# Hybrid attention and delta-rule block: one block transpose read straight from PSUM, and four steps of the per-pair chain moved to later quarters

## The reference

```python
proj = h @ w_in + b_in                      # 2048 x 14880
aq, ak, av, dq, dk_, dv_, dz, db, da, ga, gb = split_cols(proj, IN_SPLITS)
o_att = sliding_window_sink_attention(rope(aq), rope(ak), av, att_sinks)
q, k, v = causal_depthwise_conv(dq|dk_|dv_) -> silu; q, k L2-normalised per head
# gated delta rule, chunked: a = (k_beta k^T) * decay * strict, solve (I + a) sol = rhs
qk = einsum(q, k) * decay;  k_dec = k * exp(gcum[-1] - gcum)
o_dn = gated_rms_norm(o_dn, dz, dn_norm_g)
merged = sigmoid(ga) * (o_att @ w_br_att) + sigmoid(gb) * (o_dn @ w_br_dn)
h = layer_norm(ALPHA * h + merged @ w_out)
h = layer_norm(ALPHA * h + swiglu(h) + sigmoid(h @ w_ple_gate + b) * (p @ w_ple_proj))
```

## Time and profile before

| | us |
|---|---|
| median of 3 runs | 1945.42 |
| lowest, highest | 1945.41, 1946.96 |
| the profiled execution, own time | 1945.95 |
| its span in the trace | 1944.0 |
| PE busy in it | 1912.1 (98%) |
| DVE busy | 1272.8 (65%) |
| ACT busy | 1026.6 (53%) |
| turns 1 to 7 of `mixer_turn` | period 66.1 each |

### The profile page before, as it was taken

One profiled execution on the slowest core, in us unless ns is written; L12 is line 12 of the kernel. 1 busy time (PEld: TensorE's weight loads), 2 busy tenths in 40 slices (PEclk: granted clock), 3 DMA queues, 4 the chain that ended last, 5 costly groups with the idle time before them and its releaser, 6 DMA issues.

```text
span 1944.0 us, 29842 instructions
## 1 busy us (share of the span) xinstructions
PE 1912.1 (98%) x10549; PEld 1662.1 (86%) x10549; DVE 1272.8 (65%) x2348; ACT 1026.6 (53%) x2068; POOL 37.5 (2%) x79
## 2 busy tenths in 40 slices
PE   8999999999999999999999999999999999999997
PEld 7889999999999888888888788888888888888886
DVE  6657888888888756565666697555555555555555
ACT  4446666666656545455444564545444444444442
POOL 1000000000000000000000000000000000000000
PEclk9999999999999999999999999999999999999999
DMA  8665555455445557566566455655555565655552
GB/s 312 194 161 195 116 144 118 136 135 135 112 144 122 183 163 248 195 200 200 191 213 224 153 195 196 200 187 194 193 183 186 193 194 177 230 197 195 195 195 87
DMA packets 203604, 349.65 MB, mean 180 GB/s; under 512 B 6704, under 2 KB 72448, under 8 KB 202512
## 3 DMA queue, kind: packets, MB, share of 16 engines
q1 hardware_dynamic: 200272, 334.26, 52.2%
q0 software_dynamic: 3264, 14.47, 5.2%
HBM read 344.32 MB, written 2.10 MB: 178 GB/s over the span
## 4 chain that ended last, share of the span: by engine, by line
PE 89%; DVE 5%; ACT 3%; issue 3%; DMA 0%; DVEq 0%; ACTq 0%; SPq 0%
PE dense L573 23%; PE dense L574 23%; PE dense L575 23%; PE dense L561 4%; PE dense L562 4%; PE dense L563 4%; PE chain L717 1%; DVE lo L1374 1%; ACT hi L1029 1%; PE chain L799 1%; ACT sE L1207 1%; PE chain L984 0%; PE chain L726 0%; DMA raw<-in_w_in_dram 0%; PE chain L817 0%
## 5 line engine op out<-in xcount | busy, mean ns | idle before, releaser
L1374 DVE TENSOR_TENSOR lo<-raw,hi 128x512 fp32r<-128x512 f32 x1256 | 852.8, 691 | 519.8 <-ACT hi L1029 517.3
L1029 ACT ACTIVATE hi<-raw 128x512 fp32r<-128x512 f32 x1256 | 777.4, 630 | 634.6 <-PE dense L575 604.9
L573 PE MATMUL dense<-hi,xh 128*128 128x512 f32 x1376 | 539.8, 392 | 1.5 <-DVE xl L1918 1.1
L575 PE MATMUL dense<-lo,xh 128*128 128x512 f32 x1376 | 536.0, 390 | 0.0
L574 PE MATMUL dense<-hi,xl 128*128 128x512 f32 x1376 | 535.7, 389 | 0.0
L573 PEld LDWEIGHTS dense<-hi,xh 128*128 128x128 f32 x1376 | 258.7, 188 | 55.2 <-DVE xl L1918 2.0
L575 PEld LDWEIGHTS dense<-lo,xh 128*128 128x128 f32 x1376 | 258.4, 188 | 54.4
L574 PEld LDWEIGHTS dense<-hi,xl 128*128 128x128 f32 x1376 | 258.6, 188 | 52.2
L561 PE MATMUL dense<-xh,hi 128*128 128x256 f32 x1024 | 303.2, 296 | 0.0
L563 PE MATMUL dense<-xh,lo 128*128 128x256 f32 x1024 | 289.4, 283 | 0.0
L562 PE MATMUL dense<-xl,hi 128*128 128x256 f32 x1024 | 289.2, 282 | 0.0
(11 more groups left out here) (309 smaller groups left out, 1516.4 us busy)
## 6 DMA issues: line engine op xcount, KB each, us to landing
raw<-in_w_in_dram SPq DMA_DIRECT2D x116, 1024.0 KB, 5.1
raw<-in_w_ffn_gate_dram SPq DMA_DIRECT2D x44, 1024.0 KB, 5.0
raw<-in_w_ffn_up_dram SPq DMA_DIRECT2D x44, 1024.0 KB, 5.1
raw<-in_w_ffn_down_dram SPq DMA_DIRECT2D x44, 1024.0 KB, 5.0
raw<-in_w_br_att_dram SPq DMA_DIRECT2D x16, 1024.0 KB, 5.0
raw<-in_w_br_dn_dram SPq DMA_DIRECT2D x16, 1024.0 KB, 5.0
raw<-in_w_out_dram SPq DMA_DIRECT2D x16, 1024.0 KB, 4.9
raw<-in_w_ple_gate_dram SPq DMA_DIRECT2D x16, 1024.0 KB, 5.0
```

What stands on the lines that cost most here:

```text
L573: pe.matmul(o, ah, hi[:, s, :], start=(k == 0), stop=False)
L575: mm = pe.matmul(o, ah, lo[:, s, :], start=False, stop=(k == nk - 1))
L1029: act.activation(hi[:, pos.slot(n), :], raw[:, slot, off:off + 512], ACT.Copy).then_inc(sem("hi_ready"), 1)
L1374: dve.tensor_tensor(lo[:, pos.slot(n), :], raw[:, slot, off:off + 512], hi[:, pos.slot(n), :].bitcast(F32), ALU.subtract).then_inc(sem("lo ...
```

## The change

In PE's stream the turning of q goes from stage 4 to stage 6 (quarter 6 to 8). On ACT the squares of q go from stage 5 to stage 7 (quarter 7 to 9), and the copies into `Um` at stage 15 wait for `t_rows` in place of `x_prod`. On DVE the mask of q k^T goes from stage 1 to stage 4 (quarter 1 to 6), the decayed keys from stage 2 to stage 8 (quarter 2 to 10), the four transposes of neighbour blocks from stage 13 to stage 14 (quarter 15 to 16), and the transpose at stage 15 waits for `x_prod` itself and reads PSUM where it read `Um`. No instruction is added or taken away, but for waits.

```diff
--- before.py
+++ after.py
@@ chain_stage, PE
-                elif k == 4:
+                elif k == 6:
                     q_to_rows(p)
@@ chain_k, ACT
-                elif k == 5:
+                elif k == 7:
                     act.wait_ge(sem("q_rows"), p + 1)
                     act.wait_ge(sem("k_sum"), p + 1)
@@ inverse_k, ACT
                 elif k == 15:
-                    act.wait_ge(sem("x_prod"), nth("x_prod", 5, p))
+                    act.wait_ge(sem("t_rows"), p + 1)
                     for q in range(0, 4, 2):
                         r = act.activation(Um[quadrant(q), :, quadrant(q + 1)],
                                            C[quadrant(q), 0, 0:P].rearrange("p (x c) -> p x c", x=4), ACT.Copy)
@@ inverse_k, DVE
-                elif k == 13:
+                elif k == 14:
                     dve.wait_ge(sem("vu_out"), nth("vu_out", 4, p))
                     for q in range(0, 4, 2):
                         a = dve.transpose(Yz[quadrant(q + 1), 0, :, quadrant(q)], flat(VU[quadrant(q), 1]))
@@
                 elif k == 15:
-                    dve.wait_ge(sem("u_other"), p + 1)
-                    dve.transpose(Tm[quadrant(1), :, quadrant(0)],
-                                  Um[quadrant(0), :, quadrant(1)]).then_inc(sem("t_rows"), 1)
+                    dve.wait_ge(sem("x_prod"), nth("x_prod", 5, p))
+                    dve.transpose(Tm[quadrant(1), :, quadrant(0)], C[quadrant(0), 0, 0:P]).then_inc(sem("t_rows"), 1)
@@ chain_k, DVE
                 elif k == 1:
-                    dve.wait_ge(sem("E"), p + 1)
-                    dve.wait_ge(sem("QKp"), p + 1)
-                    dve.wait_ge(sem("silv"), p + 1)
-                    dve.tensor_tensor(flat(QKT[:]), C[:, 1, :], flat(Em[:]), ALU.mult).then_inc(sem("QKm"), 1)
                     dve.wait_ge(sem("k_sum"), p + 1)
@@
                 elif k == 2:
                     dve.wait_ge(sem("KK"), p + 1)
+                    dve.wait_ge(sem("E"), p + 1)
                     dve.wait_ge(sem("b_scale"), p + 1)
@@
                     a.then_inc(sem("ATc"), 1)
-                    dve.wait_ge(sem("k_sum"), p + 1)
+                elif k == 8:
                     dve.tensor_tensor(kd[:], C[:, 2, :].rearrange("p (h t c) -> p h t c", h=2, t=TT)[:, :, 0, :],
                                       each(kdecs[:, 0, ds(2 * p, 2)], 2), ALU.mult).then_inc(sem("kdec"), 1)
                 elif k == 4:
+                    dve.wait_ge(sem("QKp"), p + 1)
+                    dve.wait_ge(sem("silv"), p + 1)
+                    dve.tensor_tensor(flat(QKT[:]), C[:, 1, :], flat(Em[:]), ALU.mult).then_inc(sem("QKm"), 1)
                     inverse_root("length", row[:, 1, :], row[:, 4, :], p)
```

## The result

| | before | after |
|---|---|---|
| median, us (6 runs each) | 1945.35 | 1959.3 |
| lowest, highest | 1944.97, 1946.96 | 1957.66, 1961.86 |
| the profiled execution, own time | 1945.95 | 1961.86 |
| its span | 1944.0 | 1960.1 |
| mean granted clock of PE, share of full | 0.998 | 0.992 |

The ratio is 1.0073, 95% interval 1.0062 to 1.0083: slower by 14 us. The direction was as predicted, but 1959.3 lies above both the forecast (1956.1) and the end of its range (1958.5). Another 3 to 4 us are there that I had no term for.

A forecast was written before the change was run, and what follows sets the result against it. PE, busy 98% of the span, was taken to bound the kernel, so new pauses cost time. Seven turns of 0.60 (level 1) plus 0.93 (level 5) made 10.7 us, from 1945.42 to 1956.1 us, range 1949.5 to 1958.5.

The forecast's parts named there:

- part 3: Neighbour blocks turned a quarter later: PE pauses 1.56 us before its level-5 product, +0.93 us per turn.
- the sum: Over the loop's seven turns: 7 x (0.60 + 0.93) = 10.7 us slower, giving 1956.1 us.
- Part 1: Mask and decayed keys leave quarters 1 and 2: gain 0, upper bound 0.35 us.
- Part 2: Mask arrives in quarter 6, inside DVE's unbroken stretch: PE's level-1 product comes later, +0.60 us per turn.
- Part 4: Transpose at line 1611 reads PSUM: gain 0, as the convolution in front of it decides its start.
- a vanished wait at line 726: Sign against the forecast, which expected PE's wait there to stay, 0.7 to 1.0 us each.
- Worse than the sum: Rival: ACT's new wait or heavier quarter 9 also delays PE, up to 1 us a turn: 1963 us; chance 0.07.
- The faster rival: Neighbour blocks still in time for level 5: 0.65 us a turn, 4.6 us, 1940.8 if mask free; chance 0.09.

The follow-up runs named there:

- e9: The changed kernel with six products that nobody reads put into PE's pause before level 5: 1955.3 us, ratio 1.0052.
- e12: The changed kernel once more, unaltered, timed beside e9: 1959.79 us, ratio 1.0072.
- e4: The changed kernel with the four transposes of neighbour blocks back in quarter 15: 1948.6 us, ratio 1.0016.
- e2: From the kernel before, only the mask of q k^T moved to quarter 6, with the turning of q and its squares behind it: 1950.17 us, ratio 1.0023.
- e10: e8 with the decayed keys moved to quarter 10, as in the change: 1933.89 us, ratio 0.9942.
- e8: e7 with the last block's transpose reading PSUM and placed ahead of the convolution step in quarter 17: 1934.78 us, ratio 0.9946.
- e6: e1 with six products that nobody reads put into PE's pause before level 5: 1951.98 us, ratio 1.0032.
- e3: From the kernel before, only the last block's transpose reads PSUM and ScalarE waits for it: 1945.48 us beside 1945.53, ratio 1.0.
- e7: From the kernel before, only the two transposes into `Tm` moved to quarter 16, those into `Yz` left: 1940.94 us, ratio 0.9977.
- e1: From the kernel before, only the four transposes of neighbour blocks moved a quarter later: 1959.73 us, ratio 1.0075.
- e11: e8 with the twelve small instructions of the key lengths' inverse root moved from quarter 6 to quarter 3: 1934.37 us, ratio 0.9942.

## Why the prediction was wrong, and where it was right

- **The step that failed** is in part 3 and the sum: I priced the new pause before level 5 at its own length and nothing more. After a pause of 1.46 us (as listed) PE's granted clock falls to half for 3.4 us. Of that, 0.48 us a turn shows in the end; 0.82 falls in the time in which PE would have waited at line 726 anyway. Over seven dips that makes 3.4 us, and e9 against the two measurements of the change, less what its fillers give without the clock, makes 3.0 and 3.4. Without dips the time would be 1945.35 + 7 x 1.56 = 1956.3, inside the range and beside the forecast. The trace of before couldn't show a fall, as its longest pause in the loop is 0.82 us; that was a reason to give the unseen case a term in the range, and I gave it none.
- **Luck in the sum.** In a turn of the changed kernel without a dip (e12) the two pauses come to 0.51 + 1.05 = 1.56, where I had 0.60 + 0.93 = 1.53. The sum is so near because the two misses cancel.
- **Part 1** (no gain from the emptied quarters): right for the mask. For the keys it was off by 0.1 us a turn (e4 against e2, e10 against e8).
- **Part 2** (+0.60 at level 1): 0.63 for the mask alone (e2), 0.51 in the changed kernel, where the step that the keys' move shortens by 0.10 lies in the same stretch. The release of PE by DVE's unbroken stretch is as described.
- **Part 3** (+0.93): 1.05 in e12's turns without a dip, 0.90 in e6, where the fillers also bring level 5 and level 1 forward by some 0.2 together. The pause and its place were right. I had 0.12 too little. About half of it is that PE starts 0.13 us behind `Yz` (427.29 + 0.62 to 428.04), where I took 0.07, and the other half that the turning of `sO` follows 0.91 us later and not 0.84.
- **Part 4** (nothing): right (e3). The Trainium skill (VectorE: DVE Perf Modes, "The TRN2 errata") gives a fixed cost of 120 cycles for reading PSUM and 58 for SBUF. I went by the trace's 687 and 685 ns instead, and the traces bear that out: the transpose itself took 306 ns from PSUM and 302 from SBUF. The rule on held instructions of the same page of the Trainium skill ("Two Vector instructions with no wait between them") agrees with the traces: in e8 the first of the two transposes at line 1609, whose input and output lie in the first quadrant like the convolution's, starts at 414.43, before the convolution ends at 414.51, while those whose output lies in another quadrant wait for the end of the one before (416.65 and 416.68 in the earlier trace rows, 415.74 and 415.77 at line 1612 in e8).
- **The sign that misled.** I wrote that a vanished wait at line 726 would mean that `u_other` had held it. It vanished because PE itself had become slow: it is there in e12's two turns without a dip, and in all seven of e9.
- **The rivals.** "Worse than the sum" (0.07) was the direction, but its mechanism, ScalarE's wait and its heavier quarter 9, isn't what happened. The faster rival asked for `Yz` in time, and e7 shows that this was the right condition: with `Yz` left where it was, the time falls by 4.7 us (forecast there 4.6).

## What to carry to other kernels

When an engine that bounds the kernel gets a new pause, ask what the pause does to that engine's clock as well: here 1.06 us left the clock alone, while 1.48 brought it down, so that a turn of e1 lost 2.0 us instead of an estimated 1.1, and a few products that nobody reads, put into the pause, took the surplus away. Before a batch of instructions is moved later in an engine's queue, ask of each one who waits for it; two of these four transposes had a waiter at once and two had time, and moving only the second two gave 4.7 us where moving all four cost 14. And freeing an instruction from one engine's wait helps only if what stands in front of it in its own queue isn't waiting for the same engine.

## What the runs showed of the hardware

- PE's granted clock fell from 2.4 to 1.2 GHz 0.6 to 2.1 us after the end of a pause of 1.46 to 1.49 us in the middle of otherwise dense work, stayed down for 3.4 us (twice in e1's profile for 6.8), and did so in all seven equal turns of one profiled execution of the changed kernel and in five of another. Behind pauses of 0.82 and 1.06 us it never did, nor with PE kept busy in the pause.
- The dips add to the run-to-run spread, but don't make all of it: 4.8 us in e1 and 4.2 in the changed kernel, with 1.2 in e6, but 2.6 in e12 and, without any dip, 3.0 in e2 and 2.2 in e9.
- Reading PSUM in place of SBUF cost a transpose of 32x128 nothing to speak of: 306 ns and 302 (e3, before).
- DVE instructions of 4 columns took 0.27 and 0.40 us instead of 0.16 while GpSimd worked on its own tile in SBUF (e11); that the one causes the other is not shown.
- Not settled: why two dips in e1 lasted twice as long as the others, why level 1 comes 0.09 us sooner in e6 and 0.08 in e9 than without the fillers, and why the step behind the inverse root is 0.10 us shorter once the keys stand elsewhere.
